# Gated expert outputs split in two parts, combined by single-pass products between up chunks, with the token gather ahead of the down product

## The reference, cut to what matters

```python
uu = xb @ w_up[eid] + b_up[eid]
glu = jnp.minimum(uu[:, :D_FF], SWIGLU_LIMIT)
lin = jnp.clip(uu[:, D_FF:], -SWIGLU_LIMIT, SWIGLU_LIMIT)
act = glu * jax.nn.sigmoid(SWIGLU_ALPHA * glu) * (lin + 1.0)
yb = act @ w_down[eid] + b_down[eid]
return yb * wt[:, None].astype(yb.dtype)
...
out = jnp.zeros((T, D), ys.dtype).at[tok_buf].add(ys.reshape(P, D))
```

## Time and profile before

| | us |
|---|---|
| median of three runs | 1295.73 |
| the runs | 1295.66, 1295.73, 1298.89 |
| span of the profiled execution | 1299.7 |
| PE busy | 1211.8 (93%) |
| DVE busy | 361.8 (28%) |
| ACT busy | 259.9 (20%) |

### The profile page before, as it was taken

One profiled execution on the slowest core, in us unless ns is written; L12 is line 12 of the kernel. 1 busy time (PEld: TensorE's weight loads), 2 busy tenths in 40 slices (PEclk: granted clock), 3 DMA queues, 4 the chain that ended last, 5 costly groups with the idle time before them and its releaser, 6 DMA issues.

```text
span 1299.7 us, 14599 instructions
## 1 busy us (share of the span) xinstructions
PE 1211.8 (93%) x5802; PEld 579.9 (45%) x5802; DVE 361.8 (28%) x668; ACT 259.9 (20%) x415; POOL 36.5 (3%) x90
## 2 busy tenths in 40 slices
PE   5999999998999999999999999999999999999995
PEld 4788789893333333333333333333333333333331
DVE  3545675622112222121212121222122121212123
ACT  5463352412111111111111111111111111111112
POOL 2002400000000000000000000000000000000000
PEclk9999999998889999999999999999999999999998
DMA  8550524479889999999999999999999999999861
GB/s 296 214 198 1 178 85 146 165 286 403 345 351 377 418 413 417 413 417 412 412 419 413 420 412 419 413 417 413 418 413 418 412 417 416 412 420 371 344 255 42
DMA packets 90801, 442.27 MB, mean 340 GB/s; under 512 B 3915, under 2 KB 16787, under 8 KB 57968
## 3 DMA queue, kind: packets, MB, share of 16 engines
q1 hardware_dynamic: 57952, 312.75, 59.8%
q10 hardware_dynamic: 31760, 125.85, 24.3%
q0 software_dynamic: 1056, 3.21, 0.7%
HBM read 438.06 MB, written 3.73 MB: 340 GB/s over the span
## 4 chain that ended last, share of the span: by engine, by line
PE 89%; DVE 4%; ACT 4%; issue 2%; ACTq 1%; POOL 0%; DVEq 0%; POOLq 0%
PE ps L441 35%; PE ps L455 17%; PE ps L331 14%; PE ps L462 7%; PE ps L418 7%; ACT regionP L588 2%; DVE regionP L724 2%; PE ps L433 1%; DVE regionP L688 1%; PE ps L1702 1%; PE ps L424 1%; ACTq L611 1%; PE ps L430 1%; ACT regionP L624 1%; PE ps L1487 1%
## 5 line engine op out<-in xcount | busy, mean ns | idle before, releaser
L441 PE MATMUL ps<-regionA,regionP 128*64 128x512 f32 x1024 | 224.9, 597 | 14.0 <-DVE regionP L688 14.0
L441 PE MATMUL ps<-regionB,regionP 128*64 128x512 f32 x1024 | 226.1, 600 | 0.0
L455 PE MATMUL ps<-regionD,regionP 128*64 128x512 f32 x992 | 218.2, 592 | 0.0
L667 DVE TENSOR_TENSOR regionP<-ps,regionP 128x512 f32<-128x512 f32 x32 | 22.1, 692 | 673.4 <-PE ps L448 673.4
L441 PEld LDWEIGHTS ps<-regionA,regionP 128*64 128x64 f32 x1024 | 74.4, 138 | 155.5 <-issue 152.4
L441 PEld LDWEIGHTS ps<-regionB,regionP 128*64 128x64 f32 x1024 | 72.7, 138 | 139.5 <-issue 139.2
L455 PEld LDWEIGHTS ps<-regionD,regionP 128*64 128x64 f32 x992 | 72.2, 137 | 140.7 <-issue 140.4
L604 ACT ACTIVATE regionP<-ps 128x1024 f32<-128x1024 f32 x32 | 32.7, 1023 | 458.3 <-PE ps L441 458.3
L462 PE MATMUL ps<-regionP 128*128 128x512 f32 (+1 forms) x192 | 94.0, 613 | 19.4 <-DVE regionP L724 13.2
L418 PE MATMUL ps<-regionP 128*64 128x512 f32 x384 | 92.0, 615 | 7.1 <-ACT regionP L588 4.8
L331 PE MATMUL ps<-roundedP,roundedA 128*128 128x320 f32 x272 | 85.3, 313 | 1.3 <-DVE regionP L1335 1.3
(11 more groups left out here) (276 smaller groups left out, 1034.1 us busy)
## 6 DMA issues: line engine op xcount, KB each, us to landing
regionA<-in_w_up SPq DMA_DIRECT2D x64, 2048.0 KB, 13.2
regionB<-in_w_up SPq DMA_DIRECT2D x64, 2048.0 KB, 10.7
regionD<-in_w_down ACTq DMA_DIRECT2D x60, 2048.0 KB, 18.0
regionA<-in_w_in SPq DMA_DIRECT2D x4, 2048.0 KB, 13.9
regionB<-in_w_mk SPq DMA_DIRECT2D x4, 1024.0 KB, 9.7
regionD<-in_w_mv SPq DMA_DIRECT2D x4, 1024.0 KB, 22.7
regionD<-in_w_out SPq DMA_DIRECT2D x4, 1024.0 KB, 12.5
regionD<-in_w_mq SPq DMA_DIRECT2D x4, 1024.0 KB, 5.0
```

The costliest lines, as they stand in the source:

```text
L441: ins = pe.matmul(ps[64 * half:64 * half + 64, n_, :], XTe[:, k % 4, k // 4, :], w[:, k, 1024 * half + 512 * n_:1024 * half + 512 * n_ + 512],
L455: ins = pe.matmul(ps[64 * n_:64 * n_ + 64, 6, :], lin[:, k, :], w[:, k, 512 * n_:512 * n_ + 512], start=(k == 0), stop=(k == KT - 1))
L667: dve.tensor_tensor(glu, u[:, :, 0:SLOTS], be[:, 0:8].unsqueeze(2).broadcast_to([P, KT, SLOTS]), ALU.add).then_inc(S("glu"), 1)
```

## The change

The gate moves from the table to the expert's output. ACT reads the down result into `Y` as before, then makes `YH`, the output times the gate in the rounded type; DVE makes `YL`, the rest, `Y` times the gate less `YH`, in place of `Y`. `GT` is now a plain 0/1 table of the rounded type. `combine` takes four products per tile on rounded operands. It moves to the odd step, where each of its three tiles follows one of the first three up chunks; the bias of the down products goes the same way in step 1. The gather uses bank 7 and stands right after the up product; the down product is cut into its two halves, with the gather's four transposes between them, and the transposes of the up result come last. On ACT the copy of the gathered tokens and a wait for their transposes come ahead of the copy of the up result, because `XG` now lies in the same place as `U`. On DVE the token product comes ahead of the activation.

```diff
+        XG = U[:, 0:512]
         sg = U[:, 0:512].rearrange("p (k s) -> p k s", k=KT)
+        glu = U[:, 512:1024].rearrange("p (k s) -> p k s", k=KT)
...
+        YH = [place(YH_at, 512, 1), place(x_at, 512, 1)]
+        Y, YL = reg(x_at + 512, 1024), place(x_at + 512, 1024, 1)
...
-        GT = reg(GT_at, NT)
+        GT = place(GT_at, NT, 1)
...
         def combine(pe, i, at_bank=4):
...
-                ins = pe.matmul(ps[0:n, at_bank + n_, :], GT[:, t0:t0 + n], Y[:, 512 * n_:512 * n_ + 512],
-                                start=True, stop=True)
+                pe.matmul(ps[0:n, at_bank + n_, :], GT[:, t0:t0 + n], YL[:, 512 * n_:512 * n_ + 512], start=True, stop=False)
+                ins = pe.matmul(ps[0:n, at_bank + n_, :], GT[:, t0:t0 + n], YH[n_], start=False, stop=True)
...
             def one(e, h, pair, first, last):
...
                     up_product(pe, (upA, upB)[h], 2 * c_, 2).then_inc(S("up_done"), 1)
+                    if h == 1 and c_ < 3:
...
+                        elif c_ == 0:
+                            pe.wait_ge(S("y_read"), e - 1)
+                        if not (second and c_ == 0):
+                            pe.wait_ge(S("combined"), pair * 3 + c_)
+                        rows(pe, c_).then_inc(S("combine"), 1)
...
-                else:
-                    down(e - 1, False)
-                    pe.wait_ge(S("act"), e)
-                pe.wait_ge(S("up_read"), e + 1)
-                up_turn(pe, 0, KT).then_inc(S("up_turned"), 1)
...
                 if not last:
                     if h == 1:
                         pe.wait_ge(S("slots"), pair + 2)
-                    gather(pe, 6, 1 - h).then_inc(S("gathered"), 1)
...
+                        pe.wait_ge(S("slots_read"), pair + 1)
+                    gather(pe, 7, 1 - h).then_inc(S("gathered"), 1)
+                if not first:
+                    pe.wait_ge(S("act"), e)
+                    if not second:
+                        pe.wait_ge(S("y_read"), e - 1)
+                    down(e - 1, 0, False)
                 if not last:
                     pe.wait_ge(S("gather_read"), e + 2)
...
                     gather_turn(pe, 7).then_inc(S("gather_turned"), 1)
...
+                if not first:
+                    down(e - 1, 1, False)
+                pe.wait_ge(S("up_read"), e + 1)
+                up_turn(pe, 0, KT).then_inc(S("up_turned"), 1)
```

On ACT and DVE:

```diff
+                act.activation(GT[:, :], ps[:, 7, 0:NT], ACT.Copy).then_inc(S("slots_read"), 1)
...
-                act.activation(GT[:, :], ps[:, 7, 0:NT], ACT.Copy, scale=gate_col).then_inc(S("slots_read"), 1)
...
+                for n_ in range(2):
+                    act.wait_ge(S("y_whole"), n * 2 + n_ + 1)
+                    act.activation(YH[n_][r, :], Y[r, 512 * n_:512 * n_ + 512], ACT.Copy, scale=gate_col[r, :]
+                                   ).then_inc(S("y_high"), 1)
...
+                if not last:
+                    act.wait_ge(S("gathered"), e + 2)
+                    act.activation(XG[:, :], ps[:, 7, :], ACT.Copy).then_inc(S("gather_read"), 1)
+                    act.wait_ge(S("gather_turned"), e + 2)
                 act.wait_ge(S("up_done"), (e + 1) * 4)
...
                     act.wait_ge(S("down_done"), e * 2)
...
-                    rows_read(1 - h)
                     if not last:
                         load_down(1)
...
+                    rows_read(e - 1, 1 - h)
...
+            def rows_low(n, h):
...
+                    dve.wait_ge(S("y_high"), n * 2 + n_ + 1)
+                    ins = dve.scalar_tensor_tensor(YL[r, c0:c0 + 512], Y[r, c0:c0 + 512], gate_col[r, :], YH[n_][r, :].bitcast(F32),
+                                                   ALU.mult, ALU.subtract)
+                ins.then_inc(S("y_read"), 1)
```

More of the change, by code:

```diff
@@ L478, in moe_tensor, with down @@
             pe.wait_ge(S("moe_zero"), 2)
-            gather(pe, 6, 0).then_inc(S("gathered"), 1)
+            gather(pe, 7, 0).then_inc(S("gathered"), 1)
             pe.wait_ge(S("gather_read"), 1)
             gather_turn(pe, 7).then_inc(S("gather_turned"), 1)
[L483 to L488, removed]
-                    else:
-                        pe.wait_ge(S(f"down_in{c_}"), (e + 1) * 16)
-                    down_product(pe, wlast if last else wdn, 4 * c_, 4).then_inc(S("down_done"), 1)
+            def down(e, c_, last):
+                if last:
+                    pe.wait_ge(S(f"last_down_in{c_}"), 16)
+                else:
+                    pe.wait_ge(S(f"down_in{c_}"), (e + 1) * 16)
+                down_product(pe, wlast if last else wdn, 4 * c_, 4).then_inc(S("down_done"), 1)
             def one(e, h, pair, first, last):
                 second = isinstance(e, int) and e == 1
-                rows = down_bias if second else combine if h == 0 and not first else None
+                rows = down_bias if second else combine
                 pe.wait_ge(S("tokens_in"), e + 1)
@@ L597, in one @@
                     act.wait_ge(S("slots_turned"), pair + 1)
-                    if not isinstance(e, int) or e > 1:
-                        act.wait_ge(S("combine"), pair * 3 + 3)
+                    act.wait_ge(S("combine"), pair * 3 + 3)
                     slots_read(pair, 1)
@@ L636, in moe_act @@
                     act.wait_ge(S("gathered"), n + 1)
-                    act.activation(XG[:, :], ps[:, 6, :], ACT.Copy).then_inc(S("gather_read"), 1)
+                    act.activation(XG[:, :], ps[:, 7, :], ACT.Copy).then_inc(S("gather_read"), 1)
                     act.wait_ge(S("up_done"), (n + 1) * 4)
@@ L714, in one @@
             def one(e, h, pair, first, last):
-                second = isinstance(e, int) and e == 1
-                rows = second or (h == 0 and not first)
-                if h == 1 and not last:
-                    dve.wait_ge(S("slots_turned"), pair + 1)
-                    dve.wait_ge(S("gathered"), e + 1)
-                    slots([(e + 1, 0), (e + 2, 0)])
-                def combined(i):
-                    dve.wait_ge(S("combine"), (0 if second else pair * 3) + i + 1)
-                    n = TILES[i][1]
-                    dve.tensor_tensor(acc[0:n, i, :], ps[0:n, 4:6, :].rearrange("p b f -> p (b f)"), acc[0:n, i, :],
-                                      ALU.add).then_inc(S("combined"), 1)
-                if first:
-                    dve.wait_ge(S("Gm"), 3)
-                    dve.wait_ge(S("gates_turned"), 1)
-                dve.wait_ge(S("up_turned"), e + 1)
-                swiglu(e, e, None if first else e)
-                if rows:
-                    combined(0)
-                    combined(1)
+                if h == 1:
+                    if not last:
+                        dve.wait_ge(S("slots_turned"), pair + 1)
+                        dve.wait_ge(S("gathered"), e + 1)
+                        slots([(e + 1, 0), (e + 2, 0)])
+                    for i, (t0, n) in enumerate(TILES):
+                        dve.wait_ge(S("combine"), pair * 3 + i + 1)
+                        dve.tensor_tensor(acc[0:n, i, :], ps[0:n, 4:6, :].rearrange("p b f -> p (b f)"), acc[0:n, i, :],
+                                          ALU.add).then_inc(S("combined"), 1)
                 if not last:
@@ L737, in one @@
                     tokens().then_inc(S("tokens_in"), 1)
+                if first:
+                    dve.wait_ge(S("Gm"), 3)
+                    dve.wait_ge(S("gates_turned"), 1)
+                else:
+                    rows_low(e - 1, 1 - h)
+                dve.wait_ge(S("up_turned"), e + 1)
+                swiglu(e, e, None if first else e)
                 swiglu_end(e)
-                if rows:
-                    combined(2)
             over_experts(dve, one)
+            rows_low(E - 1, 1)
             for i, (t0, n) in enumerate(TILES):
@@ L756, in moe_dve @@
                     swiglu_end(n)
+                    rows_low(n, h)
                     if h == 1:
```

58 lines of the change are left out of this document (21 added, 37 removed).

## The result

The changed kernel takes 1286.84 us (median of five runs, 1284.24 to 1290.06), the kernel before 1296.22 beside it (five runs, 1295.66 to 1298.89): a ratio of 0.991, 95% interval 0.9885 to 0.9936, 9.4 us on the medians. Over the 51 runs of the kernel before that stand beside the experiments, the time goes with the mean granted clock of the run, from 1292.9 us at 0.991 over 1295.6 to 1297.5 at 0.989 to 1306.05 at 0.979; its profiled execution has 0.983.

A forecast was written before the change was run, and what follows sets the result against it. PE bounds the kernel at 60.61 us a pair, transfers 0.5 to 0.7 us behind. Saving 8 us to the marker and 9.6 after it, less 1 for the clock, takes 17 off 1295.7: 1279 us, range 1263 to 1291.

The forecast's parts named there:

- PE's pair of 55.4 us: PE's own time for two experts after the change, down from 60.61 us.
- The single-pass product at 0.227: Each new combination product on rounded operands takes 0.227 us; 12 per pair make 2.72 us.
- The plain-product variant: Rival: combination products not single-pass, 5.9 us a pair; PE's pair 58.6, end some 3 us longer, inside the forecast.
- The transfers' floor of 60.2 us a pair: Loading the weights of two experts, 25.17 MB, holds a pair at 60.2 us after the change.
- The rival at 1219 us: PE keeps deciding, transfers have speed in reserve: pairs of 55.4 us at 454 GB/s; chance 0.06 shared with a 435 GB/s case.
- a ceiling: Transfer rates of 410 to 426 GB/s are a limit, not a demand, whether one queue or two have work.
- What is late next: PE waits before the second down half, some 5 us a pair; distance from release to reading 21.9 us, landing 18.0.
- The terms of the sum: Savings of 8 us to the marker and 9.6 from it on, +1 for the clock: together −17 us.
- the marker: End of the down product in the step of expert 28, up to which 8 us of saving were counted.
- the same 17 off either: 17 us off the profiled span of 1299.7 gives 1282.7, off the median of 1295.7 gives 1279.
- The slower rival, by the clock: Standing 5 us before a down half slows the following up product, 2.8 us lost or up to 1399 total; chance 0.07.
- Equal wait for the removed ones (1295 us): Rival: late down pieces keep 410 GB/s in force, a pair takes 61.4 us, no change in total; chance 0.10.

The follow-up runs named there:

- Experiment 2: The kernel before with half of each down piece not loaded, PE's instructions the same: 1300.59 us (ratio 1.0021).
- experiment 1: The changed kernel with half of each down piece not loaded, PE's instructions the same: 1220.29 us (ratio 0.9406).
- experiment 3: The changed kernel with the gate applied by DVE in place and two plain products per tile, no rounded halves: 1288.46 us (ratio 0.9925).
- experiment 5: The changed kernel with SP issuing the down pieces behind the up pieces, one queue instead of two: 1286.55 us (ratio 0.991).
- 7: The changed kernel with all down weights, the first expert's too, in runs of 16 KB, on two queues: 1264.71 us (ratio 0.9743).
- experiment 8: The changed kernel with down weights in runs of 16 KB, issued by SP in the queue of the up pieces: 1275.18 us (ratio 0.983).
- experiment 11: The changed kernel with up and down weights both in runs of 16 KB, on two queues: 1251.99 us (ratio 0.9621).

## Why the prediction was right, point by point

- **The mechanism.** PE decides before, by a small distance, and the transfers after: right. Experiment 2 shows the first (half the down bytes, no gain), experiment 1 the second.
- **PE's pair of 55.4 us:** 55.1 in experiment 1. The single-pass product at 0.227: 0.23 in the chain, 0.43 for the first of each group, which is where the change of column width went (0.2 a group and three groups, where 0.6 a pair was taken). The plain-product variant was put inside the forecast: so experiment 3 measured, with 1.6 us more.
- **The transfers' floor of 60.2 us a pair:** 60.2 at 418 GB/s. The rival at 1219 us is out for this kernel. Of "a ceiling" only half is right: one queue or two make no difference (418 in experiment 5, 424 in 7 and 8), but longer runs do, to 424 and 428 GB/s. The Trainium skill, "DMA: Bandwidth & Descriptors", section "Where 436 GB/s comes from", puts the ceiling at 435; the nearest that holds over 740 us here is the 428 of experiment 11, with all weights in runs of 16 KB.
- **What is late next:** the second down half, as said. Of "some 5 us a pair", 45.6 us in 12 waits make 3.5 over the 13.1 pairs of 407–1198; in ten of the twelve the half that waited then takes 5.00 to 6.35 us instead of 3.65, which makes another 1.4. That the down queue gets a third of the shared time, and its late pieces take 28 to 30 us, was not seen: the distance of 21.9 us was set against a landing of 18.0.
- **The terms of the sum.** The down product of step 28 ends at 1164.85 instead of 1176.07: −11.2, where −8 was forecast. The bytes that the two queues had moved tell how. By 407 us the kernel after is 3.9 MB ahead, 9.3 us at 418 GB/s, where 6.9 was forecast: the hole at 325–338, which was to stay, went too. From there to the marker the rate gives 3.8 (5.3 forecast), and at the marker 0.8 MB more has been loaded, −1.9 (−4 forecast). From the marker to the end of the last down product, 1263.46, it is 98.6 us, against 106.6 before: −8.0, where −9.6 was; the difference is that product's 10.03 us, for which 8.4 was set. After it 19.4 instead of 17.1: +2.3, since the closing products run at half the clock (17.2 in experiment 8, where they have a granted clock of 1.00). So the clock after the last waits costs 3.9 us more than before, where +1, of 0 to 3, was set. The sum is −16.9 for −17 because errors of 3 us one way and 3 the other cancel, which is luck.
- **The step that failed: "the same 17 off either".** It took the 4.0 us between span and median as fixed. They are not: in the profiled execution of the kernel after, the run's own time is 1284.75 for a span of 1282.9, 1.85 apart, and in each of the 51 runs of the kernel before it is 1.7 to 1.9. So the profiled execution of the kernel before took some 1301.5 us, 5.3 above the median beside the change, while the one of the kernel after lies 2.1 below its median. Counted on medians the change is worth 9.4 us, and 1279 missed by 7.8, still inside the range; the agreement of the terms above is one between these two executions. A forecast made on one execution should have said how far that execution lies from its kernel's median, 5 to 6 us here.
- **The slower rival, by the clock:** the clock does fall after ten of the twelve waits (after 3.49 us at 1135.11 and 0.88 at 1161.15 it doesn't), but for the down half that waited (5.00 to 6.35 us; 0.57 granted over the longest), not for the up product; and that this costs nothing but at the end, because the transfers decide, is argued. The granted clock over 420–1160 is 0.97.
- **Equal wait for the removed ones (1295 us):** the time is as near to it as to 1279, but not by its mechanism: it had the ACT queue's rate in force, 410 GB/s, and the rate is 418. That the sum of the waits is equal, 45.6 for 41.7 us, is no reason of that kind. The pairs gained little (60.6 to 60.2 us); the rest came from the early holes in the transfers and from PE's shorter work at the end.

## What to carry to other kernels

When two resources lie within a per cent of each other, price the second one before the change to the first, and ask which piece will be late: the shortage should fall on the buffer with the most slack. How two queues shared the transfer engines here went with the length of their runs, so the layout of a weight in memory is also its priority. If an engine must stand just before the end, give it harmless work of just that length.

## What was not expected of the hardware

- Shares by run length, with nearly equally many packets: bytes at 2 to 1, 1 to 2, 1 to 1 and 4 to 1 for runs of 8 and 4, 8 and 16, 16 and 16, 16 and 4 KB.
- Rates with the engines at a share of 1.01 to 1.02: 418 GB/s (8 and 4 KB) and 424 (8 and 16), each the same on one queue as on two, and 428 (16 and 16, two queues).
- A slower mix by longer runs: lengthening only the larger stream cost 32 us against the kernel after (1318.93 to 1286.84).
